# Embedding product ahead of the first norm, second mixer's keys projected once, 320-row up-projections padded to three full row tiles

## What is computed

```python
merged = (gates[:, :, 0] * (o_fox @ w_up_fox[i])      # o_fox: 384 wide
          + gates[:, :, 1] * (o_sb @ w_up_sb[i])      # o_sb:  320 wide
          + gates[:, :, 2] * (o_dsa @ w_up_dsa[i]))   # o_dsa: 320 wide
x = layer_norm(DEEPNORM_ALPHA * x + merged @ w_out[i], ln1_g[i], ln1_b[i])
ffn = jnp.square(jax.nn.relu(x @ w_ff_in[i])) @ w_ff_out[i]
ple = jax.nn.sigmoid(x @ w_ple_gate[i]) * (p[i] @ w_ple[i])   # p[i]: 256 x 256
x = layer_norm(DEEPNORM_ALPHA * x + ffn + ple, ln2_g[i], ln2_b[i])
```

```python
q_x, k_x, v_x = project(hx)          # h @ w_qkv, 1024 + 256 + 256 columns
q_c, k_c, v_c = project(hc)
q_x_rot, k_x_rot = apply_rope(q_x, cos, sin), apply_rope(k_x, cos, sin)
# scores of a block of 128 queries: q_x_rot . k_x_rot in a window, q_x . k_c, and a sink
# softmax over all of them together; then p_w @ v_x + p_c @ v_c, and @ w_o
```

## Time and profile before

| | |
|---|---|
| time, median of 3 runs | 2934.86 us (2931.61 to 2936.7) |
| profiled execution, own time | 2928.99 us |
| its span | 2927.2 us |
| PE busy | 2759.3 us (94%), 17920 matmuls |
| PEld busy | 2388.4 us (82%) |
| DVE busy | 1572.0 us (54%) |
| ACT busy | 1080.9 us (37%) |
| DMA | 394.55 MB, mean 135 GB/s |
| mean granted TensorE clock | 0.97 of 2.4 GHz |

### The profile page before, as it was taken

The page is one execution under the profiler, slowest core; times in us unless marked ns, Lnnn a source line. Parts: engine busy times, 40 slices in busy tenths (PEclk is TensorE's granted clock), DMA queues, the critical chain, the costliest instruction groups (busy, mean ns, idle before and its releaser), DMA issues.

```text
span 2927.2 us, 44322 instructions
## 1 busy us (share of the span) xinstructions
PE 2759.3 (94%) x17920; PEld 2388.4 (82%) x17920; DVE 1572.0 (54%) x2309; ACT 1080.9 (37%) x1428; POOL 0.2 (0%) x4
## 2 busy tenths in 40 slices
PE   7999899999989969999989999999999999989997
PEld 6887899888779968887876688787887877967897
DVE  7676565678656564333375453333453433666665
ACT  3453453335445443222241433222232222345543
POOL 0000000000000000000000000000000000000000
PEclk9998999999899989999998999999999999989998
DMA  7645567565465734354432024444434445311563
GB/s 214 195 155 171 174 194 214 153 195 160 159 201 186 202 110 113 110 141 115 141 80 72 1 58 123 132 112 135 132 101 116 122 129 147 108 42 44 143 189 101
DMA packets 585240, 394.55 MB, mean 135 GB/s; under 512 B 43686, under 2 KB 579140, under 8 KB 584900
## 3 DMA queue, kind: packets, MB, share of 16 engines
q1 hardware_dynamic: 585028, 391.63, 46.1%
HBM read 390.54 MB, written 1.05 MB: 134 GB/s over the span
## 4 chain that ended last, share of the span: by engine, by line
PE 81%; DVE 10%; ACT 4%; DMA 2%; issue 2%; SPq 0%; DVEq 0%; ACTq 0%
PE bank L2015 81%; DVE w_lo L1190 3%; ACT w_hi L839 2%; DMA raw<-in_ffn_w_out 2%; DVE xs L1205 2%; DVE t L1205 1%; DVE h_lo L1205 0%; DVE t L1198 0%; DVE acc L1198 0%; DMA raw<-in_w_in 0%; ACT x_hi L843 0%; ACT xs L843 0%; ACT t L843 0%; DVE t L1202 0%; DMA bf<-in_b_forget 0%
## 5 line engine op out<-in xcount | busy, mean ns | idle before, releaser
L1190 DVE TENSOR_TENSOR w_lo<-raw,w_hi 128x2048 fp32r<-128x2048 f32 (+3 forms) x338 | 689.9, 2041 | 594.4 <-ACT w_hi L839 592.3
L839 ACT CAST w_hi<-raw 128x2048 fp32r<-128x2048 f32 (+3 forms) x338 | 574.8, 1701 | 803.4 <-PE bank L2015 419.2
L2015 PE MATMUL bank<-h_hi,w_hi 128*128 128x512 f32 (+1 forms) x1720 | 599.1, 348 | 23.2 <-DVE h_lo L1205 16.2
L2015 PE MATMUL bank<-h_lo,w_hi 128*128 128x512 f32 (+1 forms) x1720 | 591.9, 344 | 0.0
L2015 PE MATMUL bank<-h_hi,w_lo 128*128 128x512 f32 (+1 forms) x1720 | 591.1, 344 | 0.0
L2015 PE MATMUL bank<-x_hi,w_hi 128*128 128x256 f32 x1344 | 385.9, 287 | 33.2 <-DVE x_lo L1205 13.6
L2015 PEld LDWEIGHTS bank<-h_hi,w_hi 128*128 128x128 f32 x1720 | 326.1, 190 | 77.9 <-issue 20.9
L2015 PE MATMUL bank<-x_lo,w_hi 128*128 128x256 f32 x1344 | 377.7, 281 | 0.0
L2015 PE MATMUL bank<-x_hi,w_lo 128*128 128x256 f32 x1344 | 377.2, 281 | 0.0
L2015 PEld LDWEIGHTS bank<-h_hi,w_lo 128*128 128x128 f32 x1720 | 326.8, 190 | 39.0
L2015 PEld LDWEIGHTS bank<-h_lo,w_hi 128*128 128x128 f32 x1720 | 326.2, 190 | 37.5
(11 more groups left out here) (280 smaller groups left out, 3775.7 us busy)
## 6 DMA issues: line engine op xcount, KB each, us to landing
raw<-in_ffn_w_in SPq DMA_DIRECT2D x176, 512.0 KB
raw<-in_ffn_w_out SPq DMA_DIRECT2D x64, 704.0 KB
raw<-in_w_in SPq DMA_DIRECT2D x40, 1024.0 KB
xs<-in_mod_w SPq DMA_DIRECT2D x36, 1024.0 KB, 7.0
raw<-in_mod_w SPq DMA_DIRECT2D x36, 1024.0 KB
raw<-in_w_ff_in SPq DMA_DIRECT2D x32, 1024.0 KB
raw<-in_w_ff_out SPq DMA_DIRECT2D x32, 1024.0 KB
raw<-in_w_out SPq DMA_DIRECT2D x8, 1024.0 KB
```

The costliest lines, as they stand in the source:

```text
L839: act.copy(w_hi[s][:, w], raw[at % SLOTS][:, w]).then_inc(hi_made, c.did(hi_made))
L1190: dve.tensor_tensor(w_lo[s][:, w], raw[r][:, w], w_hi[s][:, w].bitcast(F32), ALU.subtract).then_inc(lo_made, c.did(lo_made))
L2015: ins = pe.transpose(o, l, r) if transpose else pe.matmul(o, l, r, start=start, stop=stop)
```

## The change

In the first network the `ple` chunk stands ahead of `plegate` in `MAIN`: two of its four banks come before the mean's matmul, in the rings `rt` and `rv`, and two between it and the squares' matmuls, in `rd`; four modulation products move to other chunks. The 320-row weights get a third row tile of 128 rows: an additional DMA from a constant of zeros fills rows 64 to 127 of it, two memsets clear those rows of the right operand once a layer, and all products have 128 rows. In the second mixer the keys come once, in one chunk; a new order of the heads (`swa_place`) brings each query head to the rows of its key head; the order is keys of the first half, sum, queries 0, keys of the second half, queries 1 to 3 with the rotations between them, values. The last two value tiles are inside the attention's first two steps.

The diff, cut to its core (constants' places, counts of semaphores and sizes are left out):

```diff
-        + [("out", c) for c in range(4)] + [("plegate", c) for c in range(4)] + [("ple", 0)]
+        + [("out", c) for c in range(4)] + [("ple", 0)] + [("plegate", c) for c in range(4)]
...
-MOD_AFTER = [6, 8, 10, 13, 16, 18, 20, 22, 24, 26, 28, 30, 32, 34, 36, 38, 42, 46]
+MOD_AFTER = [6, 8, 10, 13, 16, 18, 20, 22, 24, 26, 28, 30, 32, 34, 40, 42, 44, 47]
...
+def swa_place(h):
+
+    return h % 4 + 4 * (h // 8), h // 4 % 2
...
+    out["zero"] = np.zeros((P, 512), f)
...
-                        (view(slot, 3, 512)[0:HALF, 2, :], src[256:320, cols])]
+                        (view(slot, 3, 512)[0:HALF, 2, :], src[256:320, cols]),
+                        (view(slot, 3, 512)[HALF:P, 2, :], dram["constants"][HALF:P, N_FIXED + N_PHASE + N_PHASE2:])]
...
-            for q in range(2):
-                chunk(columns(qkv_w, [(DH * j, k_at + DH * (2 * q + j // 2), DH) for j in range(4)]))
+            head_at = {swa_place(h): DH * h for h in range(SWA_H)}
+            chunk(columns(qkv_w, [(0, k_at, 256)]))
+            for q in range(4):
+                chunk(columns(qkv_w, [(DH * j, head_at[2 * q + j // 2, j % 2], DH) for j in range(4)]))
             chunk(columns(qkv_w, [(0, v_at, 256)]))
...
-            for q in range(4):
-                chunk(columns(qkv_w, [(0, 256 * q, 256)]))
...
+                    if k == 0:
+                        for part in (o_hi, o_lo):
+                            dve.memset(part[HALF:P, 1, 2, :].bitcast(F32), 0.0).then_inc(v_step, c.did(v_step))
...
+                for k, (full, free) in enumerate(((t_full, t_free), (v_full, v_free), (d_full, d_free), (d_full, d_free))):
                     dve.wait_ge(gate_made, c.next(gate_made))
                     if k == 0:
                         dve.wait_ge(c.last, c.own())
-                    dve.wait_ge(d_full, c.next(d_full))
-                    tt(ple_g[:, 2 * k:2 * k + 2, :], pair(d_bank()[:, :]), ple_g[:, 2 * k:2 * k + 2, :], ALU.mult).then_inc(d_free, c.did(d_free))
+                    dve.wait_ge(full, c.next(full))
+                    b = bank[2 + k] if k < 2 else d_bank()
+                    tt(ple_g[:, 2 * k:2 * k + 2, :], pair(b[:, :]), ple_g[:, 2 * k:2 * k + 2, :], ALU.mult).then_inc(free, c.did(free))
...
+                def queries(q):
                     dve.wait_ge(c.last, c.own())
                     dve.wait_ge(d_full, c.next(d_full))
                     copy(q2[:, 2 * q:2 * q + 2, :], pair(d_bank()[:, :])).then_inc(d_free, c.did(d_free))
-                bump(q_ready)
-                for q in range(2):
-                    rotate(kd[:, 2 * q:2 * q + 2, 0:S], kd[:, 2 * q:2 * q + 2, 0:S])
-                for q in range(4):
-                    rotate(q2rot[:, 2 * q:2 * q + 2, :], q2[:, 2 * q:2 * q + 2, :])
-                soft_attention(SWA_UNITS, SCALE, ow_hi, ow_lo, swa_end, True)
+
+                def turn(dst, src):
+                    rotate(dst, src, s_full, s_free, s_bank, t3[:, 1, :])
+
+                def turn_queries(q):
+                    turn(q2rot[:, 2 * q:2 * q + 2, :], q2[:, 2 * q:2 * q + 2, :])
+
+                passed()
+                queries(0)
+                for j in range(2):
+                    dve.wait_ge(a_full, c.next(a_full))
+                    copy(kd[:, j, :], a_bank()[:, :]).then_inc(a_free, frees_gate_bank())
+                passed()
+                passed()
+                queries(1)
+                turn(kd[:, :, 0:S], kd[:, :, 0:S])
+                turn_queries(0)
+                passed()
+                queries(2)
+                turn_queries(1)
+                passed()
+                queries(3)
+                turn_queries(2)
+                turn_queries(3)
+                passed()
+
+                def values(s):
+                    if s in (0, 2):
+                        dve.wait_ge(d_full, c.next(d_full))
+                        copy(vw[:, s:s + 2, :], pair(d_bank()[:, :])).then_inc(d_free, c.did(d_free))
+
+                soft_attention(SWA_UNITS, SCALE, ow_hi, ow_lo, swa_end, True, values)
...
-                                rows = slice(0, HALF if b and k == 2 else P)
                                 cols = slice(P * (2 * q + t), P * (2 * q + t) + P)
-                                product(d[:, S * t:S * t + S], [z[rows, k, cols] for z in w],
-                                        (o_hi[rows, b % 2, k, :], o_lo[rows, b % 2, k, :]), k == 0, k == 2,
+                                product(d[:, S * t:S * t + S], [z[:, k, cols] for z in w],
+                                        (o_hi[:, b % 2, k, :], o_lo[:, b % 2, k, :]), k == 0, k == 2,
...
+                pe.wait_ge(p_hi_made, c.next(p_hi_made))
+                pe.wait_ge(p_lo_made, c.next(p_lo_made))
+                w = parts(chunk(), 2, D)
+
+                def ple(qs):
+                    for q in qs:
+                        ring, give = ((rt, t_full), (rv, v_full), (rd, d_full), (rd, d_full))[q]
+                        pe.wait_ge(ring.free, ring.awaited())
+                        b = ring.claim()
+                        for t in range(2):
+                            tile(b[:, S * t:S * t + S], w, P * (2 * q + t), None, x_tiles(p_hi, p_lo, 2), give=give if t else None)
+
+                ple(range(0, 2))
+                layer_norm_sums(lambda qs: ple(range(2, 4)) if qs[0] == 0 else None)
+                done(m)
+                m += 1
...
-                pe.wait_ge(rd.free, rd.all_used())
...
+                    if s == 3:
+                        pe.wait_ge(rd.free, rd.all_used())
...
+                made = c.seen.get(h_lo_made, 0)
+                c.seen[h_lo_made] = made + 2 * KT
+                copied = {}
+
+                def keys(w, s):
+                    for k in range(KT):
+                        pe.wait_ge(h_lo_made, made + KT * s + k + 1)
+                        for x in range(2):
+                            product(kb[x][:, HALVES[s]], [t[:, k, P * x:P * x + P] for t in w],
+                                    (h_hi[:, k, HALVES[s]], h_lo[:, k, HALVES[s]]), k == 0, k == KT - 1,
+                                    a_full if s and k == KT - 1 else None)
+
+                def queries(q):
                     w = parts(chunk(), KT, 256)
+                    b = claim(rd)
                     for j in range(2):
                         tile(b[:, S * j:S * j + S], w, P * j, None, x_tiles(h_hi, h_lo, KT), give=d_full if j else None)
+                    copied[q] = rd.used
+
+                def turn_queries(q):
+                    pe.wait_ge(d_free, c.value(d_free, copied[q] + 1))
+                    rotation([q2[:, 2 * q + j, :] for j in range(2)], rs, s_full)
+
+                wk = parts(chunk(), KT, 256)
+                kb = [claim(ra) for _ in range(2)]
+                keys(wk, 0)
+                half_sum(1)
+                queries(0)
+                keys(wk, 1)
+                used_chunk(0)
                 flush()
+                used_chunk(1)
+                queries(1)
+                used_chunk(2)
+                pe.wait_ge(ra.free, ra.all_used())
+                rotation([kd[:, j, 0:S] for j in range(2)], rs, s_full)
+                turn_queries(0)
+                for q in range(2, 4):
+                    queries(q)
+                    used_chunk(q + 1)
+                    turn_queries(q - 1)
+                wv = parts(chunk(), KT, 256)
+                vb = []
+
+                def values(t):
+                    if t % 2 == 0:
+                        vb.append(claim(rd))
+                    toks = slice(P * t, P * t + P)
+                    for k in range(KT):
+                        product(vb[-1][:, S * (t % 2):S * (t % 2) + S], (h_hi[:, k, toks], h_lo[:, k, toks]), [z[:, k, :] for z in wv],
+                                k == 0, k == KT - 1, d_full if t % 2 and k == KT - 1 else None)
+                    if t == 3:
+                        used_chunk(5)
+
+                values(0)
+                turn_queries(3)
+                values(1)
+                pe.wait_ge(roped, c.next(roped, 5))
 
                 def score(b, h, part):
+                    (t, half), toks, g = swa_place(h), slice(P * part, P * part + P), h // (2 * SWA_H // SWA_KV)
+                    hp = slice(HALF * half, HALF * half + HALF)
+                    mm(b[:, 0:S], q2rot[hp, t, toks], kd[hp, g, 0:S], True, True)
+                    mm(b[:, S:2 * S], q2[hp, t, toks], kd[hp, g, S:2 * S], True, True, s_full)
...
+                soft_attention(SWA_UNITS, score, weigh, lambda s: values(s + 2) if s < 2 else None)
```

More of the change, by code:

```diff
@@ L241, in ring_order @@
     put(["main"] * (LAYERS * CHUNKS1))
-    for unit, between in (((0, 0), 13), ((0, 1), 0), ((1, 0), 11), ((1, 1), 2)):
+    for unit, between in (((0, 0), 13), ((0, 1), 0), ((1, 0), 10), ((1, 1), 2)):
         put([kind for kind, _ in ffn_stream(unit)] * 2 + ["main"] * between)
@@ L990, in _ @@
                     a_at[0] += 1
-                passed()
-                m += 1
```

(21 more changed lines are left out.)

99 lines of the change are left out of this document (32 added, 67 removed).

## The result

The changed kernel takes 2887.43 us (median of 4 runs, 2883.29 to 2897.41) against 2934.38 (4 runs); the ratio is 0.9845, 95% interval 0.9816 to 0.9875. Forecast were 57, and 2878; the measured time lies inside the range.

What follows compares the result with a forecast made beforehand. TensorE was taken as the bound, with 81% of the chain that ended last. Up-projections 18.7, embedding product 12.2 and second mixer 26 summed to a gain of 57, giving 2878 against 2934.86; range 2865 to 2896.

Steps and rivals of the forecast that it cites:

- With the clock back after the first bank, counted from 256.40: two slow tiles 3.8: Third branch's up-projection: the first two tiles pass at the low clock, ending at 3.8 us, then the full clock returns.
- the next step: Third branch's up-projection: VectorE falls behind; its order puts the first output chunk's end at 21.0 us.
- Rival 2: Third branch's clock stays at 1.2 GHz: 9.6 for 13.7, gain 53, 2882; chance 0.14.
- The wait of 1.4 for `w_lo`: Behind the first network's norm: TensorE waits 1.4 us for VectorE's weight remainder, needed one plegate chunk earlier.
- 3.1 later: First network's norm: the first plegate product comes 3.1 us later, as the moved embedding product delays the squares.
- The wait ahead of the second query chunk: Second mixer, before the first score: a new wait of 2.6 us for the next chunk's remainder, ending at 2534.5.
- 0.7 for a low clock behind the wait: Second mixer: 0.7 us taken off the gain for a low clock behind the wait of 2.6.
- The two late value tiles (5.8) fill the first steps, where TensorE waits: Second mixer's attention: two value tiles use idle time; the fifth score comes only about 1 us later against the first.
- should be over: Second mixer's attention: the low clock ends by the fifth score, saving 2.3 and 0.3 us on the next two units.
- Rival 1: Weight conversions take the freed time, w_lo is next to be late: gain 40, 2895; chance 0.15.
- Rival 3: No wait behind the norm or in the second mixer, VectorE off the third branch's path: gain 70, 2865; chance 0.07.
- rivals 4 and 5: Rival 4: 256-byte query pieces late, 2887, chance 0.03; rival 5: second mixer's attention stays at low clock, 2951, chance 0.02.

Runs made afterwards that it cites:

- pad_second_branch: Kernel before with only the second branch's up-projection products padded to 128 rows, the third branch's third product left at 64; 2917.53 us, ratio 0.9941.
- pad_third_branch: Kernel before with only the third branch's up-projection products padded to 128 rows; 2921.89 us, ratio 0.9962.
- late_low_half: Changed kernel, VectorE makes the weights' low half behind the sums of the third branch's second half instead of ahead of them; 2879.31 us.
- mods_moved: Kernel before with only the last modulation products moved, to behind chunks 40, 42, 44, 47; 2936.25 us, ratio 1.0005.
- norm_and_flush: Changed kernel, second plegate chunk prepared ahead of the first norm, and the chunk-reporting matmul in flush leaves its bank's mark unchanged; 2877.68 us.
- values_ahead: Changed kernel with all four value tiles ahead of the second mixer's attention instead of two inside its first two steps; 2889.03 us.
- third_chunk_early: Changed kernel, second mixer's third chunk (queries 1) rounded and its remainder made between the norm's two halves instead of behind the second; 2880.51 us.
- all_four: Changed kernel with the edits of late_low_half, norm_and_flush and third_chunk_early together; 2868.10 us, ratio 0.9775.

## Why the prediction was right, and where it was not

**Up-projections: right in size, wrong in its mechanism.** Forecast 18.7, measured 19.1 by the medians and 19.9 by U on average. The step "With the clock back after the first bank, counted from 256.40: two slow tiles 3.8" did not happen, because the clock was never lost. I had taken the alternation of 128 and 64 rows inside the third branch for what makes the clock low there. `pad_second_branch` shows alternation at full clock in that place, and `pad_third_branch` a recovery inside the branch with no alternation. Whether the clock falls is decided ahead of the third branch, by the second branch's padding. The Trainium skill (TensorE: Matmul & The Clock Gate, What's actually happening) says that the clock is set by how busy the engine has been recently. That the stretch ahead of the fall matters agrees with it; that TensorE stood idle longer in that stretch where the clock stayed up (2.8 us against 2.0) does not, if busy is what the trace counts. Its rule that activity releases the throttle agrees with `pad_third_branch`, and still does not fit, busy and slow for 20 us. Why alternation keeps a low clock low when it does not lower a high one is open. The size came out because the next step was right: VectorE is the limit once TensorE is fast. TensorE's 8.8 us instead of 10.3 changed little, and with 11.6 in `pad_second_branch` the output chunks end as early. Forecast 21.0 to the end of the first output chunk, measured 20.7 and 20.8; `late_low_half` shows that VectorE's order was that limit. The second branch gave 2.1 a layer for 2.5 (its tile was to be a quarter shorter, 1.09 for 1.44, not the fifth that the text says). Rival 2 (a clock that stays at 1.2 GHz) is out.

**Embedding product: the stage gave more, the kernel less.** Forecast 12.2. The wait of 1.4 for `w_lo` came as worked out (1.41). The mis-sized term is the "3.1 later" of the first plegate product. It was worked out from the second layer's rows and used for both; there the product moved by 2.9, but in the first layer only by 1.3, because the squares ran at the low clock there before (5.4 us against 3.7). That second layer was the exception: of the ten layers in the five traces that have the old order, nine have slow squares, and the changed kernel has none. So E gained 7.7 and 7.1 on average (144.0 and 143.4 in those five, 136.3 in the six kernels whose norm is the changed kernel's), 14.8 in all. Outside the stage some of it went. The stretch from the end of the first network's products to the second mixer, which the change doesn't touch, is 1450.6 on average in five kernels without the moved product and 1453.4 in a sixth, and 1455.4 in eight with it: 4.8 more, nearly all of it TensorE's waits for `xs`. What is left, 10.0, is what the medians give the product alone, 10.4 (5.9 to 12.9 by its interval). By its waits, `mods_moved` rules out the modulation products' places. Why `in_ffn_w_out` lands later in those kernels was not found; I had costed everything outside the three stages at nothing. By these averages the three stages gained 19.9, 14.8 and 19.5, 54 in all, or 49 after the 4.8, against 47 by the medians.

**Second mixer: 26 forecast, 17 measured (19.5 by the traces).** This is the step that failed. Up to the first score 25.0 were forecast, less 0.7 for a low clock, and 22.0 came (77.2 on average before, 55.2 after). The wait ahead of the second query chunk was found in the right place, but too short: 3.3 instead of 2.6, since `flush` had marked the bank as used and TensorE waited for the copy of the first queries too, which `norm_and_flush` took away. The "0.7 for a low clock behind the wait" was 1.5 to 2.5 in three of four traces and nothing in the fourth. And the keys now claim banks of `ra`, which VectorE frees last: TensorE stands 3.27 ahead of the first key chunk (it was 1.17 and then 1.58 for `w_lo`), which by the timelines costs 0.7 net; this was read, not tested.

In the attention I forecast 1.6 gained, and 2.5 were lost (94.5 on average in six traces, 97.1 in four). The step "The two late value tiles (5.8) fill the first steps, where TensorE waits" is wrong: `values_ahead` shows the same total. The step that the low clock "should be over" from the fifth score on is the other. Before, the attention began at the low clock and kept it for 12 to 22 us. In the changed kernel it begins at 1.00, and the clock falls 12 to 13 us after the first score, for 3.4 to 6.8 us, in all four traces. In `norm_and_flush`, `third_chunk_early` and `all_four` the same waits stand there, the clock stays up, and the attention takes 94.3. So some 2.8 of the loss against the forecast are this low clock, whose cause no run shows, and the other 1.4 are tiles that fill nothing. `third_chunk_early` gets 7 back by the medians with the order of the conversions alone, 2.8 of which may be the attention's clock.

**The rivals.** None names what happened. Rival 1 (conversions take the freed time, gain 40) is a little nearer to the 47 measured than the forecast of 57 is, but not by its mechanism: the second branch lost nothing to them, the second mixer's wait for `w_lo` was as forecast (2.46 when it stood alone, for 2.6), and the larger part of the shortfall is in the attention, where TensorE waits for no `w_lo`. Rival 3 did not come, and neither did rivals 4 and 5: no wait for the 256-byte pieces is in the chain, and at 2575.84 and after, the attention's scores are 2.7 apart.

## What to carry to other kernels

Where a stretch runs at the low clock, look at what the engine did before it, and change one stretch at a time: half of this padding did all the work here. When TensorE gets faster, the next limit is the order of the helper engine's queue: here moves of single operations in that order, with one bank's mark, were worth some 19 us by the medians, nearly twice what the moved product gave. Work put into an engine's waits is free only if nothing that waits stands behind it in the same queue.

## What the runs showed of the hardware that I had not expected

The same 768 matmuls of the second feed-forward product, without a wait and at a granted clock of 1.00, took either 87.2 or 90.6 us, in the layers of one execution too (windows 450.00 and 960.00 above). That is 0.1135 or 0.1180 a matmul. Of the 28 layers in the 14 traces 9 have the shorter time and 19 the longer one, none another, and nothing in the traces says which it will be. It moves a layer by 3.4 us. The two traces of the changed kernel are 18.9 us apart; 3.4 of this is one such product, and 4.2 the second mixer with its clock behind short waits. So a profiled execution's span says little about an edit of this size.
